# Expert gates of a PEER layer: from one-hot products to a scatter through DRAM, and part of one token tile's value product by gathered rows

## Chip, cores and metric

One core of one Trainium2 chip runs the whole kernel as one program. The metric is device time in microseconds (us) of a run, from several runs of the same compiled kernel.

## What is computed

The reference is one encoder block on 256 tokens of width 2048 in float32: a token-mixing sublayer (pooling, attention, gates), then a retrieval sublayer. The change is in the retrieval sublayer:

```python
q = jnp.einsum('bsd,de->bse', x, wq).reshape(B, S, PEER_HEADS, 2, PEER_HALF)      # 8 heads
s1 = jnp.einsum('bshc,kc->bshk', q[..., 0, :], keys1)                             # 128 keys each
s2 = jnp.einsum('bshc,kc->bshk', q[..., 1, :], keys2)
v1, i1 = lax.top_k(s1, 16);  v2, i2 = lax.top_k(s2, 16)
cand = v1[..., :, None] + v2[..., None, :]                                        # 256 candidates
vals, pos = lax.top_k(cand, 16)
ids = take_along_axis(i1 * 128 + i2, pos);  gates = softmax(vals)                 # 16 picks a head
h = jnp.einsum('td,tkd->tk', xb, u_tab[ids])
out = jnp.einsum('tk,tkd->td', gelu(h) * gates, v_tab[ids])                       # 128 picks a token
```

The kernel computes the two last lines densely: h for all 16,384 experts and all 256 tokens, gelu, a multiplication by a gate matrix that is zero where a token did not pick the expert (gates of one expert picked by several heads add up), and a product with the whole of v_tab.

## The kernel before

**Units.** All weights stream from HBM in units of 128 x 1024 float32 (512 KB). SyncE loads unit u into one of four RAW slots once DVE has converted unit u - 4 (load, L302); ACT rounds it to float32r into HI (L436); DVE writes the rest, RAW - HI, into LO (conv, L720; two slots, so the conversion of u waits for the end of unit u - 2); TensorE multiplies hi by hi, hi by lo and lo by hi (use, L1178 on). The order is written out by hand: while TensorE does unit n, ACT converts n + 3 and DVE n + 1. The 774 units come in stages: v, qk, pool, gate, grp, branch, wout, plew, wq, pleg, u (256 units), vtab (256 units).

**t_unit** (L1194, L1195, L1199) keeps weights stationary: 16 hi matmuls and 8 lo matmuls with 256 token columns each. **n_unit** (L1212, L1219) keeps tokens stationary: a unit is one half (1024 columns) of a row block, and does for each of two token tiles two hi passes and one lo pass over two 512-column pieces: 8 + 4 matmuls of 512 columns.

**u stage.** Two units give one "chunk" of 128 experts (one value of i2, all i1): h for 128 experts x 256 tokens in PSUM. ACT applies gelu into BUF[:, k, :] (L650) for the first 64 chunks, while DVE does the top-k searches, one step tk0 to tk7 behind each conversion (L978 to L1041). After 64 chunks the picks are turned by TensorE, and for the last 64 chunks each unit is followed by the one-hot products of two tokens: DVE builds two one-hot tiles per token (onehots, L1079, L1081), TensorE multiplies them (gate_products, L1448) into the token's 128 x 128 gate matrix, and DVE multiplies BUF with it (spread, L1092, L1096). Chunks not yet reached hold 1.0, which two POOL memsets wrote (L410, L412).

**vtab stage.** For each key k ACT and DVE split BUF[:, k, :] into a_hi and a_lo (L683, L1131), and n_unit multiplies with the 128 rows v_tab[:, k, :], two units (halves) per key, adding up in all eight PSUM banks until the end.

**POOL** also scales the residual and adds the gated embedding (L403 to L407), stores it in DRAM (L408) and brings it back in pieces late in vtab (L421, L423). DVE then adds it, and the last layer norm follows. In the pool stage DVE sums windows (pool_sums, L818) in buffers that lie where the change puts its zeros.

## Time and profile before

| | us |
|---|---|
| median of 3 runs | 2414.81 (2414.21 to 2416.8) |
| the profiled execution's own time | 2416.51 |
| its span, first to last instruction | 2414.8 |
| TensorE busy | 2307.8 (96%) |
| DVE busy | 1538.1 (64%) |
| ACT busy | 1028.5 (43%) |
| POOL busy | 72.5 (3%) |

The granted TensorE clock is 0.982 of full speed on average. The queue of SyncE moved 412.14 MB (54.1% of the time of the 16 DMA engines), the queue of POOL 12.71 MB; the mean over the span is 176 GB/s. Shares are means over stages; a busy TensorE means that matmuls followed one another, not that each ran at its peak. A duration of an engine's instruction includes pipelining, so that neighbours overlap by a few hundredths of a us.

### The profile page before, as it was taken

How to read it: one execution, taken by the hardware profiler on the slowest of the kernel's cores; microseconds unless marked ns; L12 is line 12 of the kernel's file. 1: busy time of each engine (PE TensorE's matmuls, PEld its weight loads, DVE VectorE, ACT ScalarE, POOL GpSimd, SP SyncE). 2: the span in 40 equal slices, each digit the busy share in tenths (PEclk: the TensorE clock that was granted, in tenths of full speed). 3: DMA queues.
4: the chain of work that ended last, by engine and by line, in shares of the span. 5: the costliest groups of instructions: out<-in, count | busy, mean ns of one | idle time of the engine just before them, and what ended most of it. 6: DMA issues, size and time to landing. Idle time of an engine off the chain costs nothing.

```text
span 2414.8 us, 45807 instructions
## 1 busy us (share of the span) xinstructions
PE 2307.8 (96%) x15504; PEld 2135.9 (88%) x15504; DVE 1538.1 (64%) x2726; ACT 1028.5 (43%) x1390; POOL 72.5 (3%) x64
## 2 busy tenths in 40 slices
PE   4999999899899989999999999999999999999996
PEld 4999999897699879999999999999788888888885
DVE  4446655565653568777779898989555555555556
ACT  2444455554444443444443333333444444444442
POOL 0000000000010040000000000000000000000000
PEclk9999999999999999999999999999999999999998
DMA  6655555455544555555554445444566666666663
GB/s 178 189 182 164 172 178 168 155 181 177 192 142 156 187 166 172 182 182 182 181 177 131 160 157 159 157 157 157 182 193 194 202 205 201 201 202 202 206 193 123
DMA packets 116576, 425.28 MB, mean 176 GB/s; under 512 B 13840, under 2 KB 13856, under 8 KB 115520
## 3 DMA queue, kind: packets, MB, share of 16 engines
q1 hardware_dynamic: 112608, 412.14, 54.1%
q0 software_dynamic: 3936, 12.71, 2.2%
q8 instruction: 20, 0.33, 0.1%
q14 instruction: 12, 0.10, 0.0%
HBM read 418.50 MB, written 6.29 MB: 176 GB/s over the span
## 4 chain that ended last, share of the span: by engine, by line
PE 90%; DVE 5%; DMA 3%; issue 1%; ACT 1%; DVEq 0%; SPq 0%; ACTq 0%
PE ps L1212 24%; PE ps L1199 17%; PE ps L1194 17%; PE ps L1195 17%; PE ps L1219 12%; PE ps L1448 2%; DMA raw<-in_w_in 2%; DVE w_lo L720 1%; DMA ln_gb<-in_ln_in 1%; DVE bn L733 0%; DVE x L739 0%; DVE tk_ab L1022 0%; PE ps L1320 0%; PE ps L1390 0%; DVE x L745 0%
## 5 line engine op out<-in xcount | busy, mean ns | idle before, releaser
L720 DVE TENSOR_TENSOR w_lo<-raw,w_hi 128x1024 fp32r<-128x1024 f32 x774 | 957.7, 1239 | 713.7 <-PE ps L1219 418.0
L436 ACT ACTIVATE w_hi<-raw 128x1024 fp32r<-128x1024 f32 x774 | 820.5, 1061 | 1061.2 <-DMA raw<-in_peer_v 384.2
L1194 PE MATMUL ps<-x_t_hi,w_hi 128*128 128x256 f32 x3328 | 835.9, 289 | 21.0 <-ACT v_t L486 12.5
L1195 PE MATMUL ps<-x_t_lo,w_hi 128*128 128x256 f32 x3328 | 820.9, 284 | 0.0
L1194 PEld LDWEIGHTS ps<-x_t_hi,w_hi 128*128 128x128 f32 x3328 | 641.7, 193 | 25.9 <-ACT w_hi L436 15.9
L1195 PEld LDWEIGHTS ps<-x_t_lo,w_hi 128*128 128x128 f32 x3328 | 642.4, 193 | 0.0
L1199 PE MATMUL ps<-x_t_hi,w_lo 128*128 128x256 f32 x3328 | 472.1, 285 | 13.5 <-DVE w_lo L720 13.5
L1199 PEld LDWEIGHTS ps<-x_t_hi,w_lo 128*128 128x128 f32 x3328 | 433.3, 194 | 14.8 <-DVE w_lo L720 14.7
L1212 PE MATMUL ps<-w_hi,x_t_hi 128*128 128x512 f32 x1024 | 315.8, 390 | 3.0 <-DVE x_t_lo L1131 3.0
L1212 PE MATMUL ps<-w_hi,x_t_lo 128*128 128x512 f32 x1024 | 316.1, 390 | 0.0
L1219 PE MATMUL ps<-w_lo,x_t_hi 128*128 128x512 f32 x1024 | 274.1, 389 | 0.0
L1212 PEld LDWEIGHTS ps<-w_hi,x_t_hi 128*128 128x128 f32 x1024 | 192.5, 188 | 43.1 <-issue 3.2
L1219 PEld LDWEIGHTS ps<-w_lo,x_t_hi 128*128 128x128 f32 x1024 | 192.6, 188 | 40.2
L1212 PEld LDWEIGHTS ps<-w_hi,x_t_lo 128*128 128x128 f32 x1024 | 192.5, 188 | 40.1
L1096 DVE TENSOR_TENSOR experts<-ps,experts 128x512 f32 (+1 forms) x64 | 87.6, 1369 | 13.2 <-DVE experts L1092 13.1
L1212 PE MATMUL ps<-w_hi,a_hi 128*128 128x512 f32 x272 | 87.5, 403 | 7.7 <-DVE a_lo L932 3.7
L1081 DVE TENSOR_SCALAR onehots<-iota,i_t,gate_t 128x128 f32<-128x128 bf16 x256 | 92.6, 362 | 0.0
L1079 DVE TENSOR_SCALAR onehots<-iota,i_t 128x128 f32<-128x128 bf16 x256 | 77.5, 303 | 17.7 <-DVE experts L1096 13.2
L1212 PE MATMUL ps<-w_hi,a_lo 128*128 128x512 f32 x272 | 87.4, 403 | 0.0
L1448 PE MATMUL ps<-onehots 128*128 128x128 f32 x512 | 79.0, 277 | 5.2 <-DVE onehots L1081 5.2
L1219 PE MATMUL ps<-w_lo,a_hi 128*128 128x512 f32 x272 | 75.3, 399 | 0.0
L1448 PEld LDWEIGHTS ps<-onehots 128*128 128x128 f32 x512 | 69.3, 194 | 5.6 <-DVE onehots L1081 5.6
(204 smaller groups left out, 1313.8 us busy)
## 6 DMA issues: line engine op xcount, KB each, us to landing
raw<-in_u SPq DMA_DIRECT2D x256, 512.0 KB, 4.6
raw<-in_peer_v SPq DMA_DIRECT2D x256, 512.0 KB, 4.9
raw<-in_w_in SPq DMA_DIRECT2D x128, 512.0 KB, 4.6
raw<-in_branch SPq DMA_DIRECT2D x32, 512.0 KB, 3.9
raw<-in_wout SPq DMA_DIRECT2D x32, 512.0 KB, 3.7
raw<-in_wq SPq DMA_DIRECT2D x32, 512.0 KB, 3.8
raw<-in_pleg SPq DMA_DIRECT2D x32, 512.0 KB, 3.8
x<-in_x SPq DMA_DIRECT2D x2, 1024.0 KB, 6.2
```

Of the source, the lines that this page charges most:

```text
L436: nc.scalar.activation(HI[:, u % 4, :], RAW[:, u % 4, :], ACT.Copy).then_inc(hi_ready, 1)
L720: v.tensor_tensor(LO[:, u % 2, :], RAW[:, u % 4, :], HI[:, u % 4, :].bitcast(F32), ALU.subtract) \
L1079: ch.tag(v.tensor_scalar(OH[:, j % 2, r, 0, :], IOTA[:, :], I1T[:, bass.ds(t, 1)], None, ALU.is_equal))
L1081: ins = v.tensor_scalar(OH[:, j % 2, r, 1, :], IOTA[:, :], I2T[:, bass.ds(t, 1)], GATET[:, bass.ds(t, 1)], ALU.is_equal, ALU.mult)
L1096: v.tensor_tensor(dst, PS[:, 4 + c, :].rearrange("p (t e) -> p t e", t=4), dst, ALU.mult) \
L1194: mm(o, w(HI, u % 4)[:, k, :], xh[:, ks * half + k, :], start=(s and k == 0), stop=False)
L1195: mm(o, w(HI, u % 4)[:, k, :], xl[:, ks * half + k, :], start=False, stop=False)
L1199: r = mm(o, w(LO, u % 2)[:, k, :], xh[:, ks * half + k, :], start=False, stop=(e and k == 7))
L1212: mm(nbank(tt, 2 * half + q), stn[:, tt * P:(tt + 1) * P], HI[:, u % 4, q * 512:(q + 1) * 512], start=(first and s == 0), stop=False, skip ...
L1219: r = mm(nbank(tt, 2 * half + q), ah[:, tt * P:(tt + 1) * P], LO[:, u % 2, q * 512:(q + 1) * 512], start=False, stop=last, skip_group_chec ...
L1448: r = mm(PS[:, 4 + c, o:o + P], OH[:, j % 2, t, 0, :], OH[:, j % 2, t, 1, :], start=True, stop=True)
```

## The change

**Search.** The top-k search does both token tiles at once, in 16 stages per head (tk0 to tk15), one behind each conversion from unit 7 of wq on; products and index arithmetic are on floats. It yields cell addresses (ID, in SBUF) for the two tiles and row addresses (IDV) for the second.

**Gates.** In three batches of heads (0 to 2, 3 and 4, 5 to 7), ACT exponentiates, DVE normalises, and then DVE sums for every pick the gates of equal cells over the heads up to that batch's end: one scalar_tensor_tensor with accumulation per pick and tile, five behind a conversion (merge_gates). As equal cells get their sum, POOL scatters the sums plainly: per head and tile 16 indirect DMAs of 128 cells of 4 bytes into a gate array of 8 MB per tile in DRAM. That array is set to zero by 16 DMAs of POOL from the start of qk on. pool_sums waits for the last of them.

**u stage.** All 128 chunks go through gelu on ACT, which also writes the second tile's half of each to DRAM (64 KB). The one-hots, their products, the spreading, the turned picks and the memsets of 1.0 are gone. At unit 192 SyncE waits until all is scattered, and then reads the gates of a chunk back (two DMAs of 64 KB) into three slots, behind the load of the unit; DVE multiplies two chunks behind each conversion from step 196 on, and the last eight after the last conversion.

**vtab stage.** For the second token tile the last 768 columns are left out of the dense product: odd units do 6 matmuls of 512 columns and 3 of 256. In their place POOL gathers, for each of 128 picks, a row piece of 768 columns for each of the tile's 128 tokens, and the gelu value of the pick; DVE multiplies and adds into ACC, spread over keys 10 to 127. The residual comes back in 1 MB pieces at pick 64. DVE's loops over u and vtab are written out.

```diff
+PICKS = HEADS * TOPK
+BATCHES = ((0, 3), (3, 5), (5, 8))
...
+G_SLOTS = 3
+GC = 768
+DC = D - GC
+REST = DC - UNIT
+ROWS = 7
+PICKS_FROM = 10
+G_FROM = 195
...
+def gated_by(n):
+
+    return max(0, min((n - G_FROM) * 2, n // 2 - 2))
...
+            def chunk_gates(k):
+
+                if k >= G_SLOTS:
+                    sp.wait_ge(g_mult, k - G_SLOTS + 1)
+                for tt in range(NT):
+                    sp.dma_start(GR[:, k % G_SLOTS, tt * P:(tt + 1) * P], gates_dram[tt][k]
+                                 ).then_inc(g_in[k % G_SLOTS], 16)
...
+                if name == "vtab":
+                    for j in range(4):
+                        load(None, 4, b + j, src(name, None, j // 2, j % 2))
+                        for k in range(gated_by(2 * NK - 5 + j), gated_by(2 * NK - 4 + j)):
+                            chunk_gates(k)
+                    for k in range(gated_by(2 * NK - 1), NK):
+                        chunk_gates(k)
+                    first = 1
...
+                if name != "u":
+                    continue
+                for tt in range(NT):
+                    sp.wait_ge(scattered[tt], 16 * PICKS)
+                for j in range(4 * last, 2 * n):
+                    load(None, 4, b + j, src(name, None, j // 2, j % 2))
+                    for k in range(gated_by(j - 5), gated_by(j - 4)):
+                        chunk_gates(k)
...
+            pool.wait_ge(zero_ready, 1)
+            pool.wait_ge(unit_done, BASE["qk"])
+            for n in range(16):
+                pool.dma_start(gates_dram[n // 8][n % 8 * 16:n % 8 * 16 + 16].rearrange("k p e -> p k e"), ZERO[:, :, :]
+                               ).then_inc(zero_out, 16)
...
-            pool.wait_ge(n_act, 16)
+            cells = [gates_dram[tt].rearrange("k p t -> (k p t)").unsqueeze(1) for tt in range(NT)]
+            def residual():
+                pool.wait_ge(n_act, 16)
+                for tt in range(NT):
+                    step(nc.gpsimd.tensor_tensor(SIG[:, tt, :], SIG[:, tt, :], PW[:, tt, :], ALU.mult))
+                    step(nc.gpsimd.tensor_tensor(X0[:, tt, :], X0[:, tt, :], SIG[:, tt, :], ALU.add))
+                    pool.dma_start(spill[tt], X0[:, tt, :]).then_inc(spill_out, 16)
...
+            pool.wait_ge(zero_out, 16 * 16)
+            for h0, h1 in BATCHES:
+                for h in range(h0, h1):
+                    pool.wait_ge(gates_ready, h + 1)
+                    for tt in range(NT):
+                        if h:
+                            pool.wait_ge(scattered[tt], 16 * TOPK * h)
+                        for p in range(TOPK * h, TOPK * (h + 1)):
+                            pool.indirect_dma_start(out=cells[tt], out_offset=bass.IndirectOffsetOnAxis(
+                                ap=ID[:, tt, p:p + 1], axis=0), in_=GSC[:, tt, p:p + 1], in_offset=None
+                                ).then_inc(scattered[tt], 16)
+                    if h == 0:
+                        residual()
             for tt in range(NT):
...
+                pool.wait_ge(scattered[tt], 16 * PICKS)
+            hidden_cells = hidden.rearrange("k p t -> (k p t)").unsqueeze(1)
+            table = a["peer_v"].rearrange("a b (c d) -> (a b c) d", d=256)
+            for n in range(4):
+                pool.wait_ge(h_out[n], 16 * NK // 4)
+
+            def picked(p):
+                pool.indirect_dma_start(out=HP[:, p:p + 1], out_offset=None, in_=hidden_cells,
+                                        in_offset=bass.IndirectOffsetOnAxis(ap=ID[:, 1, p:p + 1], axis=0)
+                                        ).then_inc(h_in[p // TOPK % 2], 16)
+
+            for p in range(TOPK):
+                picked(p)
+            pool.wait_ge(unit_done, BASE["vtab"])
+            for p in range(PICKS):
+                if p >= ROWS:
+                    pool.wait_ge(row_used, p - ROWS + 1)
+                pool.indirect_dma_start(out=ROW[p % ROWS][:, :], out_offset=None, in_=table,
+                                        in_offset=bass.IndirectOffsetOnAxis(ap=IDV[:, p:p + 1], axis=0)
+                                        ).then_inc(row_in[p % ROWS], 16)
+                if p + TOPK < PICKS:
+                    picked(p + TOPK)
+                if p == 64:
+                    pool.wait_ge(al_ready, KD + 2 + KD + 32)
+                    for tt in range(NT):
+                        pool.dma_start(RES2[:, tt, :], spill[tt]).then_inc(res_in, 16)
+                    for x in range(2):
+                        pool.dma_start(LNG2[:, x, :], bass.AP(tensor=a["ln2"].tensor, offset=x * D,
+                                                              ap=[[0, P], [1, D]])).then_inc(ln_in[2], 16)
...
+                    act.wait_ge(act_evac, val(i, 4, 80 + c + 1))
+                    if i is not None:
+                        act.wait_ge(h_out[c], i * 16)
+                    nc.scalar.dma_start(hidden[k].rearrange("k p t -> (k p) t"),
+                                        BUF[:, k, P:S].rearrange("p k t -> p (k t)")).then_inc(h_out[c], 16)
...
+                act.wait_ge(g_mult, val(i, 4, c + 1))
...
-                dve.wait_ge(const_ready, 3)
+                dve.wait_ge(const_ready, 4)
...
+            scores = lambda h, tt, f: SC[:, 2 * h + tt, f, :]
+            first = lambda h: slice(TOPK * h, TOPK * h + 8)
+            second = lambda h: slice(TOPK * h + 8, TOPK * (h + 1))
+
...
+            def merge_gates(b, n):
+
+                h0, h1 = BATCHES[b]
                 ch.wait()
...
+                if (NT * TOPK * h0 + 5 * n) // (NT * TOPK):
+                    dve.wait_ge(gates_ready, (NT * TOPK * h0 + 5 * n) // (NT * TOPK))
+                for m in range(NT * TOPK * h0 + 5 * n, min(NT * TOPK * h0 + 5 * n + 5, NT * TOPK * h1)):
+                    h, tt, p = m // (NT * TOPK), m // TOPK % NT, m // (NT * TOPK) * TOPK + m % TOPK
+                    width = TOPK * h1
+                    ins = v.scalar_tensor_tensor(out=SAME[:, m % 5, 0:width], in0=IDF[:, tt, 0:width],
+                                                 scalar=IDF[:, tt, p:p + 1], in1=GATE[:, tt, 0:width],
+                                                 op0=ALU.is_equal, op1=ALU.mult, accum_out=GSC[:, tt, p:p + 1])
+                    if m % (NT * TOPK) == NT * TOPK - 1:
+                        ins.then_inc(gates_ready, 1)
+                    else:
                         ch.tag(ins)
...
+            def gated(k):
+
+                dve.wait_ge(h_out[k % 4], 16 * (k // 4 + 1))
+                dve.wait_ge(g_in[k % G_SLOTS], 16 * NT * (k // G_SLOTS + 1))
+                v.tensor_tensor(BUF[:, k, :], BUF[:, k, :], GR[:, k % G_SLOTS, :], ALU.mult).then_inc(g_mult, 1)
+
+            st = stage("pleg", KD + 2, gt_block, AH, AL)
+            for n in range(32):
+                conv(None, 4, BASE["wq"] + n + DVE_LEAD)
+                search(n - 7)
+            for n in range(32):
+                if n % 2 == 0:
+                    st(None, n // 2)
+                conv(None, 4, BASE["pleg"] + n + DVE_LEAD)
+                if n < 27:
+                    search(25 + n)
+                elif n == 27:
+                    gates_out(0)
+                else:
+                    merge_gates(0, n - 28)
+            done, found = 0, 52
+            for n in range(2 * NK):
+                conv(None, 4, BASE["u"] + n + DVE_LEAD)
+                if n == 53:
+                    gates_out(1)
+                if n == 117:
+                    gates_out(2)
+                if n < 16:
+                    merge_gates(0, 4 + n)
+                elif 54 <= n < 67:
+                    merge_gates(1, n - 54)
+                elif 118 <= n < 138:
+                    merge_gates(2, n - 118)
+                elif found <= STAGES * HEADS:
+                    search(found)
+                    found += 1
+                for k in range(done, gated_by(n)):
+                    gated(k)
+                done = gated_by(n)
+            for k in range(done, NK):
+                gated(k)
...
+            def pick(p):
+
+                g = p // TOPK
+                if p % TOPK == 0:
+                    sl = slice(p, p + TOPK)
+                    dve.wait_ge(h_in[g % 2], 16 * TOPK * (g // 2 + 1))
+                    ch.link(v.tensor_tensor(HP[:, sl], HP[:, sl], GATE[:, 1, sl], ALU.mult))
+                dve.wait_ge(row_in[p % ROWS], 16 * (p // ROWS + 1))
+                if p == 0:
+                    ins = v.tensor_scalar(ACC[:, :], ROW[0][:, :], HP[:, 0:1], None, ALU.mult)
+                else:
+                    dve.wait_ge(row_used, p)
+                    ins = v.scalar_tensor_tensor(out=ACC[:, :], in0=ROW[p % ROWS][:, :], scalar=HP[:, p:p + 1],
+                                                 in1=ACC[:, :], op0=ALU.mult, op1=ALU.add)
+                ins.then_inc(row_used, 1)
...
+                upto = max(0, (k - PICKS_FROM + 1) * PICKS // (NK - PICKS_FROM))
+                if made < upto:
+                    pick(made)
+                    made += 1
+                if k + 2 < NK:
+                    a_lo(None, k + 2)
+                if k + 1 < NK:
+                    conv(None, 8, vb + 2 * k + 1 + DVE_LEAD)
+                while made < upto:
+                    pick(made)
+                    made += 1
+
+
+            dve.wait_ge(res_in, 16 * 2)
+            dve.wait_ge(row_used, PICKS)
+            ch.tag(v.tensor_tensor(RES2[:, 1, DC:D], RES2[:, 1, DC:D], ACC[:, :], ALU.add))
+            dve.wait_ge(ln_in[2], 16 * 2)
             for half in range(2):
 
                 dve.wait_ge(unit_done, UNITS - 1 + half)
                 for tt in range(NT):
...
             for tt in range(NT):
                 stats(RES2, tt)
@@ -1205,19 +1361,24 @@
 
                 half = u % 2
 
+                def pieces(tt):
+                    if u >= BASE["vtab"] and half and tt:
+                        return [(q, min(512, REST - 512 * q)) for q in range(2) if REST > 512 * q]
+                    return [(0, 512), (1, 512)]
+
                 def his():
                     for tt in range(NT):
                         for s, stn in enumerate((ah, al)):
-                            for q in range(2):
-                                mm(nbank(tt, 2 * half + q), stn[:, tt * P:(tt + 1) * P],
-                                   HI[:, u % 4, q * 512:(q + 1) * 512], start=(first and s == 0), stop=False,
+                            for q, w in pieces(tt):
+                                mm(nbank(tt, 2 * half + q)[:, 0:w], stn[:, tt * P:(tt + 1) * P],
+                                   HI[:, u % 4, q * 512:q * 512 + w], start=(first and s == 0), stop=False,
                                    skip_group_check=True)
 
                 def los():
                     for tt in range(NT):
-                        for q in range(2):
...
                         pe.wait_ge(act_evac, i * 4 + (80 + j // 2 - 1))
 
                         pe.wait_ge(n_act, 12 if j == 0 else 16)
                     t_unit(i, 8, BASE["u"] + j, 2 * (j // 2 % 2), j % 2, XH, XL)
-            pe.wait_ge(act_evac, 80 + TOPK_CHUNKS)
-
```

## Rows read from the trace of the kernel before

**Rows 1.** Windows: stretch, its length; busy us (instructions) per engine; PEclk, DMA share, GB/s
```profile
10.00:20.00 10.00, 0.01 (x1) 0.00 (x0) 7.38 (x12) 3.10 (x4) 0.00 (x0) 1.00 0.95 384
...
910.00:1240.00 330.00, 330.00 (x2739) 330.00 (x2739) 261.18 (x847) 139.92 (x171) 0.00 (x0) 0.99 0.58 183
...
1275.00:1690.00 415.00, 414.02 (x3490) 413.83 (x3490) 373.70 (x752) 153.15 (x185) 0.00 (x0) 1.00 0.50 157
...
1705.00:2380.00 675.00, 675.00 (x2980) 558.92 (x2979) 346.09 (x373) 300.62 (x372) 8.60 (x16) 1.00 0.65 199
```

**Rows 2.** Chain of waits, pieces at seams: start us, us, what
```profile
871.36 0.38 PE ps L1194
...
909.51 2.08 PE ps L1199 x8
...
1257.10 0.97 PE ps L1199 x8
...
1690.18 0.97 PE ps L1199 x8
...
1694.61 3.29 PE ps L1212 x8
...
1704.66 1.81 PE ps L1212 x8
1706.47 0.91 PE ps L1219 x4
```

**Rows 3.** DVE groups, whole span; the last one from 1720 to 2350 us only
```profile
L720 DVE TENSOR_TENSOR w_lo<-raw,w_hi 128x1024 fp32r<-128x1024 f32 x774 | 957.7, 1239 | 713.7 <-PE ps L1219 418.0 <-PE ps L1199 260.0 <-ACT w_hi L436 30.3
...
L1131 DVE TENSOR_TENSOR x_t_lo<-experts,x_t_hi 128x256 fp32r<-128x256 f32 x128 | 53.6, 419 | 1.1 <-ACT x_t_hi L683 1.1
...
L745 DVE SCALAR_TENSOR_TENSOR x<-x,rstd,ln_gb 128x1024 f32<-128x1024 f32 x8 | 9.7, 1282 | 0.1
...
L829 DVE SCALAR_TENSOR_TENSOR pool_w<-pool_w,pool_in 128x512 f32<-128x512 f32 x4 | 2.8, 692 | 0.1
...
L720 DVE TENSOR_TENSOR w_lo<-raw,w_hi 128x1024 fp32r<-128x1024 f32 x232 | 284.3, 1225 | 307.2 <-PE ps L1219 304.5 <-ACT w_hi L436 2.7
```

**Rows 4.** Timeline of POOL: start us, us, instruction
```profile
21.05 1.10 POOL L369 DMA_DIRECT2D bias_by_rel_dram<-bias_by_rel  x1 [14.72 <-ACT bias_by_rel L474]
...
884.32 4.58 POOL L406 TENSOR_TENSOR ple_gate<-ple_gate,p_w 128x2048 f32<-128x2048 f32 x1
...
899.13 8.63 POOL L410 MEMSET experts<- 128x10240 f32 x1 [3.82 <-DMA residual_dram<-x]
...
1903.24 0.54 POOL L421 DMA_DIRECT2D residual<-residual_dram  x1 [24.71 <-ACT x_t_hi L683]
```

**Rows 5.** DMA issues: queue, count, KB each, median us from issue to landing
```profile
raw<-in_u SPq DMA_DIRECT2D x256, 512.0 KB, 4.6
raw<-in_peer_v SPq DMA_DIRECT2D x256, 512.0 KB, 4.9
...
ln_gb<-in_ln_in SPq DMA_DIRECT2D x2, 1024.0 KB, 12.1
bias_by_rel_dram<-bias_by_rel POOLq DMA_DIRECT2D x1, 2048.0 KB, 46.2
...
bias<-bias_by_rel_dram POOLq DMA_DIRECT2D x8, 64.0 KB, 2.1
```

**Rows 6.** Chain of waits early in the v stage
```profile
36.74 30.21 DMA raw<-in_w_in
```

**Rows 7.** Timeline of DVE beside the POOL operations of rows 4
```profile
885.72 4.28 DVE L720 TENSOR_TENSOR w_lo<-raw,w_hi 128x1024 fp32r<-128x1024 f32 x1
...
899.97 7.82 DVE L1021 TENSOR_SCALAR tk_ab<-tk_pos 128x16 uint32<-128x16 uint32 x1
...
1903.32 1.23 DVE L720 TENSOR_TENSOR w_lo<-raw,w_hi 128x1024 fp32r<-128x1024 f32 x1 [1.50 <-PE ps L1219]
```

More of the change, by code:

```diff
@@ L436, in conv, with run @@
                 nc.scalar.activation(HI[:, u % 4, :], RAW[:, u % 4, :], ACT.Copy).then_inc(hi_ready, 1)
-            def run(name, iters, per, slots, pre=None, start=0, stop=None):
+            def run(name, iters, per, slots, pre=None, start=0, stop=None, peel=False):
                 b = BASE[name]
@@ L966, in _ @@
             xt_lo(1)
-            run("wq", 8, 4, {})
-            run("pleg", 8, 4, {}, pre=stage("pleg", KD + 2, gt_block, AH, AL))
             def settle():
```

425 lines of the change are left out of this document (184 added, 241 removed).

## Prediction, made before the change was run

> **What bounds the kernel now.** I read the table of windows first [rows 1]. In the three long stretches TensorE (PE) is busy for all but 1 us in 1,420, and at the full granted clock; VectorE (DVE) is busy 79% of the first half of the u stage, 90% of its second half and 51% of the vtab stage. The chain of waits [rows 2] gives the periods. In vtab a unit is 8 matmuls in 1.81 us and 4 in 0.91 us: 2.72 us, or 227 ns for 512 columns. In the first half of u, the 120 units between the ends at 911.59 (909.51 + 2.08) and 1258.07 (1257.10 + 0.97) take 2.887 us each, or 120 ns for a matmul of 256 columns. The two sizes are 107 ns apart, so a column costs 0.417 ns and a matmul 13 ns besides. The second half of u (128 units up to 1691.15) takes 3.38 us a unit, because two tokens' one-hot products follow every unit. So the kernel is bound by matmul columns, except at seams. PE stands between 1691.15 and 1694.61, and the first 8 units of u, from 871.36 to 911.59, take 40.2 us where 8 periods are 23.1: 17 us lost.
>
> **Term 1, one-hot products go.** The second half of u with its seam ran 1258.07 to 1691.15, 433.1 us; 128 units at 2.887 us are 369.5. Gain **63.6 us**. The one-hots, the spreading multiply and the transposes of the picks go with it.
>
> **Term 2, columns go in vtab.** Each odd unit loses three 512-column matmuls (680 ns), and three shrink from 512 to 256 columns (3 x 107 = 320 ns): 1.00 us per key. 128 keys give **128 us**, and a key (two units) then takes 5.44 - 1.00 = 4.44 us. This is the gain only if nothing else needs over 4.44 us.
>
> DVE in vtab [rows 3]: two conversions of 1.239 us, one a_lo of 0.419, and 1.085 gathered multiply-adds per key (128 spread over 118 keys). Its scalar_tensor_tensor took 692 ns for 512 and 1,282 ns for 1,024 columns, so 987 ns for 768. Sum 2.48 + 0.42 + 1.07 = 3.97 us of 4.44. Of the 307 us that DVE idled before its conversions in that stage, 304.5 were for PE, so it has room, though after the change only a tenth.
>
> DMA in vtab: a key's loads are 1.049 MB and its 1.085 rows of 128 x 3,072 bytes 0.427 MB: 1.475 MB in 4.44 us, 332 GB/s. The trace bounds the ceiling: 384 GB/s at 95% share between 10 and 20 us, and 199 GB/s at a share of 0.65, which stretched to 1.0 is 306 [rows 1]. At 384 it costs nothing; at 306 a key takes 4.82 us, 118 x 0.38 = 45 us. The first row is a rate that was reached, the second only a proportion, so I take **+15 us**, a third of the way.
>
> **Term 3, gates by scatter.** POOL issues 256 scatters of 128 cells in u, and in vtab 128 row gathers and 112 one-word gathers (16 before them). No row has an indirect DMA. The nearest are plain ones: 0.54 us on POOL for one of 128 rows, 1.10 us for one of 1,024 [rows 4]; none bounds it from above, which is rival B. I take 1.1 us. In vtab 2.17 per key need 2.4 of 4.44 us. In u the last three heads become ready from step 124 on, and SP holds its loads at step 192 until all has landed: 96 scatters in about 64 x 2.887 = 185 us, so 1.9 us each is allowed. Cover for both: nothing.
>
> DVE in u: search and merging. The largest step is a 1,024-element operation beside the conversion, 2 x 1.24 = 2.48 us of 2.887; a merge step has five 128-wide instructions of some 0.25 us (by the same line), 1.25 + 1.24. Nothing; cover some 0.4 us a unit, and in pleg less. ACT's 128 writes of 64 KB and its table loads lie in ACT's idle time.
>
> **Term 4, the zero fill.** 16 DMAs write 16.8 MB from the start of qk, and pool_sums waits for the last some 35 units later: 35 x 2.887 = 101 us, 166 GB/s beside loads of 183. The sum, 349, lies under 384. Below: nothing. Above: a 2 MB write from POOL landed after 46.2 us [rows 5] and a load beside it held the chain for 30.2 us [rows 6], though that write reads only eight partitions. I take **+8 us** (0 to 40).
>
> **Term 5, start of u.** POOL's four large tensor operations and a memset held DVE: a conversion took 4.28 us beside a 4.58 us POOL operation and a 16-element tensor_scalar 7.82 us beside an 8.63 us memset [rows 4, 7]. The memsets of 1.0 go, the four operations move behind the 32 scatters of head 0, beside search steps. I keep two thirds of the 17 us: **-5 us** (0 to -10).
>
> **Term 6, gate reads in the tail of u.** This is what hides badly. In steps 196 to 255 DVE multiplies two chunks per unit; their four reads of 64 KB stand on SP's queue right behind the 512 KB load of the same step, in three slots. The load goes out when a conversion ends (time x); the chunks are wanted after the next conversion. Let L be the time until they have landed and P the period. DVE then multiplies twice (0.84), converts (1.24) and spends some 0.1 on waits, and this must end at x + 2P: 2P = L + 2.2. P stays 2.887 if L is under 3.6 us. Bounds for L: a 64 KB read on POOL's queue lands in 2.1 us, a load of u in 4.6 [rows 5]. On one queue later ones do land later: the ln_gb rows, issued behind two x loads, took 12.1 us. I take the load's 4.6 + 0.3: P = 3.55, 60 x 0.66 = **+40 us** (0 to 60). The last eight chunks come after the last step, three slots per round of 2.1 us of landing, 0.42 of multiplying and some waits, about 3 us: 8 us in all, then a_lo(0): the stop of 3.46 us between u and vtab grows to some 13: **+10 us**.
>
> The Trainium skill (DMA: Bandwidth & Descriptors, Queues, rings and completion order) says that each DMA engine consumes one ring's descriptors in order. By that rule L is the load's own landing and more, and the term stands; without it L would be the lone 64 KB read's and the term zero. The ln_gb row agrees with the rule.
>
> At the end, the gathered sum's add goes before the last units are ready and two adds shrink: nothing.
>
> **Sum.** 2414.8 (span) - 63.6 - 128 + 15 + 8 - 5 + 40 + 10 = 2291. The profiled execution took 2416.5 us around its span of 2414.8; the median of the runs is 2414.81, the span by chance, so the sum is taken for the median: **2290 us**. About 0.2% (5 us) is what a measurement tells from no change.
>
> **Rivals.**
> A. *Indirect DMAs hold DVE* (ends slower). For: a POOL tensor operation kept a two-input DVE operation waiting until it ended [rows 4, 7]. Against: a plain POOL DMA from 1903.24 to 1903.78 left the conversion begun at 1903.32 at its usual 1.23 us. If each held DVE for h us: in vtab (taking 0.08 us off each instruction where they overlap) 3.7 + 2.17h against 4.44, over 118 keys; in u 1.35h against some 0.5 us of room over 190 units. That is 118 x (2.17h - 0.74) + 190 x (1.35h - 0.5), or 512h - 182: with h = 1.1, 381 us, 2670 us in all. It decides from h = 0.6 on. Chance 0.10.
> The Trainium skill (SBUF — State Buffer, Who interferes with whom) says that a DVE instruction with two SBUF inputs contends with a GpSimd instruction that reads SBUF. An indirect DMA reads its offsets there, so this rule speaks against the change; the POOL tensor operations agree with it, and no row shows an indirect DMA.
> B. *POOL is too slow.* At t us per indirect DMA: 256 x (t - 2.05) in vtab and 96 x (t - 1.9) before step 192; t = 2.5 gives 173 us, 2463 us. Slower from 2.3 us on. For: nothing measured; against: 0.54 and 1.10. Chance 0.06.
> C. *DMA becomes vtab's bound.* At 306 GB/s 30 us more than summed, 2320; at 270 GB/s a key takes 5.46 us, 120 us in place of 15: 2395. For: loads of peer_v already land later than those of u (4.9 against 4.6 us, [rows 5]) and gathers are shorter; against: 384. Chance 0.22.
> D. *The gate reads are hidden*: L under 3.6, the fill free, 384 GB/s: 2290 - 40 - 8 - 15 = 2227 us. Chance 0.14.
>
> **How the numbers follow.** Forecast 0.48, within 2250 to 2350. Those 0.48, C and D are faster; A and B mostly slower, with a sliver around no change and a piece of them (h near 0.5) still faster. Faster 0.82, same 0.03, slower 0.15. The range, 2225 to 2430, reaches over D, C and the first of B, and leaves out A with some of B.
>
> **What the profile would show.** Term 1: 24-matmul units at 2.88 us through u up to step 195. Term 2: odd vtab units at 1.72 us, PE at 100%; if DVE is longer than 1.24 us in its conversions, A; if ACT waits for raw<-in_peer_v before PE stands, C; if DVE waits for rows while DMA has room, B. Term 6: DVE before the chunk multiply waiting for DMA, P near 3.5 us. Term 4: ACT waiting for raw in qk, or DVE for zero_out. I am wrong if u's tail runs at 2.88 us, or if vtab's keys differ from 4.44 us by over 0.3.

## The result, and the profile after

The changed kernel was timed in four sets of executions, each beside the kernel before. They don't agree:

| set | changed kernel, us | before beside it, us | ratio, 95% interval |
|---|---|---|---|
| first (the one that the prediction was made for) | 2571.77 median of 4 (2527.32 to 2588.30) | 2415.81 | 1.0524 [1.0415, 1.0633] |
| second (e9) | 2292.61 median of 5 (2289.75 to 2294.55) | 2413.61 | 0.9495 [0.9482, 0.9507] |
| third (e12) | 2287.44 median of 4 (2284.63 to 2287.80) | 2414.44 | 0.9472 [0.9456, 0.9488] |
| fourth (e18) | 2289.06 median of 2 (2287.12 to 2291.01) | 2414.76 | 0.9480 [0.9461, 0.9499] |

In the first set the executions of 2585.74 and 2588.30 us count as slow, and the ratio is that of the two others (2527.32 and 2557.81 us).

The prediction was 2290 (2225 to 2430), faster. Against the first set it is wrong in sign and 282 us off; the three later ones, of the same kernel unedited, lie within 3 us of it. The three later sets ran on three different chips of this kind; on which the first ran is not recorded. The edited kernels below ran in these sets and in two more, on two further chips. So there are two questions: what took 280 us in the first set, and whether 2290 came out for the right reasons.

**Where the first set's time went.** Windows of its profile (stretch, its length; busy us and instructions of PE, PEld, DVE, ACT, POOL; PEclk, DMA share, GB/s):

```profile
100.00:200.00 100.00, 100.00 (x837) 100.00 (x836) 41.67 (x34) 43.07 (x60) 14.41 (x14) 1.00 0.95 346
...
940.00:1000.00 60.00, 27.99 (x154) 24.25 (x154) 22.65 (x71) 6.33 (x8) 48.04 (x41) 0.67 0.32 98
1000.00:1034.00 34.00, 4.71 (x13) 3.44 (x12) 2.09 (x5) 1.06 (x1) 26.04 (x27) 0.50 0.06 16
1050.00:1150.00 100.00, 100.00 (x836) 100.00 (x835) 76.28 (x209) 46.11 (x55) 0.00 (x0) 1.00 0.63 194
1400.00:1480.00 80.00, 34.44 (x164) 27.95 (x163) 14.75 (x66) 7.13 (x8) 61.65 (x61) 0.61 0.16 45
```

Read PE against POOL: where POOL has nothing to do (1050 to 1150) TensorE is busy all the time, as before; in the worst stretch of POOL's scatters (1000 to 1034) it gets 13 matmuls done in 34 us. Inside such a stretch the timeline shows each of them by itself (start, us, instruction, idle time before it):

```profile
1466.23 0.37 PE L1355 MATMUL ps<-x_t_hi,w_lo 128*128 128x256 f32 x1 [1.73 <-issue]
1467.22 0.96 POOL L479 DMA_INDIRECT gates_dram<-cell_gates,cell_ids  x1 [0.30 <-issue]
1468.32 0.29 PEld L1355 LDWEIGHTS ps<-x_t_hi,w_lo 128*128 128x128 f32 x1 [3.21 <-issue]
1468.49 0.97 POOL L479 DMA_INDIRECT gates_dram<-cell_gates,cell_ids  x1 [0.30 <-issue]
1469.03 0.37 PE L1355 MATMUL ps<-x_t_hi,w_lo 128*128 128x256 f32 x1 [2.43 <-issue]
```

These are matmuls of the same unit on operands that are long there; no semaphore stands between them. PE waits 1.7 to 2.4 us ahead of nearly each with nothing in the profile to wait for ("issue"), while POOL's scatters keep their steady 1.27 us (0.97 and 0.30), and the DMA engines are nearly idle. The granted clock is down at 0.50 there (the 1.2 GHz level), after PE had been waiting; a matmul takes 0.37 us instead of some 0.28. DVE's longest waits from 900 to 1550 us name no one the profile knows ("remote"); its ordinary wait, for PE, stands below them:

```profile
DVE w_lo L815 <- remote: 250.5, 23, 46.6
DVE w_lo L815 <- PE ps L1355: 88.5, 99, 2.7
```

(us in total, times, longest.) The slowness doesn't begin with a burst. POOL issues the first scatter of the third burst at 1395.50; PE keeps its pace of 0.12 us a matmul for 14 us and ten scatters, and this is its first stop:

```profile
1409.78 0.28 PE L1351 MATMUL ps<-x_t_lo,w_hi 128*128 128x256 f32 x1 [0.35 <-issue]
```

From there the stops grow. POOL issues the last scatter of head 6 at 1479.94, and from 1490 on PE is busy all the time again, until head 7's scatters slow it in the same way.

From 874.9 to the end of its last matmul at 1905.5, u took 1031 us; in e12 it took 783. These 248 us, and some 20 at the start of vtab, where POOL's gathers come in a burst and the chain holds 6.95, 5.09 and 12.45 us of "another core or an unknown queue" between 1928 and 1956, are but for 3 us the whole difference of the two spans (2556.1 against 2285.4). I call it the crawl.

**The same kernel without it.** Windows of e12, columns as above; POOL's scatters fill 1275 to 1375 in just the same way, and PE does not notice:

```profile
875.00:975.00 100.00, 93.86 (x765) 93.05 (x764) 81.77 (x250) 40.19 (x50) 78.69 (x55) 0.98 0.63 194
...
1275.00:1375.00 100.00, 100.00 (x836) 100.00 (x835) 43.59 (x41) 43.74 (x53) 78.75 (x70) 1.00 0.65 194
...
1450.00:1650.00 200.00, 177.02 (x1374) 167.33 (x1374) 111.19 (x171) 67.75 (x86) 0.00 (x0) 1.00 0.78 232
...
1690.00:2190.00 500.00, 490.24 (x2262) 400.54 (x2261) 394.01 (x439) 257.58 (x324) 282.99 (x229) 1.00 0.92 324
...
1860.00:1960.00 100.00, 99.38 (x463) 81.72 (x462) 82.21 (x92) 51.91 (x66) 60.54 (x48) 1.00 0.91 323
1960.00:2060.00 100.00, 92.69 (x417) 74.26 (x416) 73.35 (x82) 47.92 (x60) 56.44 (x48) 0.98 0.91 333
2060.00:2160.00 100.00, 99.30 (x464) 82.04 (x464) 82.10 (x92) 52.73 (x66) 59.17 (x47) 1.00 0.92 326
```

Its chain of waits (start, us, what), at the start of u, in u's tail, at the seam and at the end:

```profile
870.48 1.58 ACT ple_gate L741 x3
...
1562.74 1.23 DVE w_lo L815
1563.99 0.33 SPq L327
...
1564.37 0.43 SPq L334
...
1564.84 4.10 DMA gate_chunks<-gates_dram
...
1569.03 0.44 DVE experts L1221
...
1569.48 0.32 SPq L334
...
1569.85 2.65 DMA gate_chunks<-gates_dram
...
1572.93 1.23 DVE w_lo L815
...
1653.49 1.23 PE ps L1355 x8
...
1655.59 0.38 ACT experts L749
1655.96 12.07 issue
1668.03 3.75 PE ps L1373 x8
...
2257.02 0.60 PE ps L1380 x3
```

With [rows 2] and the last unit of before (which ended at 2392.8) this gives the budget, stage by stage:

| stretch | before | e12 | difference | predicted |
|---|---|---|---|---|
| to the first matmul of u | 871.4 | 872.1 | +0.7 | +8 |
| u | 819.8 | 782.7 | -37.1 | -28.6 |
| stop between u and vtab | 3.5 | 13.3 | +9.8 | +10 |
| vtab | 698.2 | 589.6 | -108.6 | -113 |
| from the last matmul | 22.0 | 27.8 | +5.8 | 0 |
| span | 2414.8 | 2285.4 | -129.4 | -123.6 |

### The profile page after: what moved, and what is told of

Its sections match the earlier page's. It is cut to its first block, busy times and chain, and to the rows that moved or that the text cites. A ratio compares the mean times of both kernels' runs of the same rounds, so it can differ in the third digit from the quotient of the medians.

```text
span 2556.1 us, 43127 instructions
## 1 busy us (share of the span) xinstructions
PE 2224.6 (87%) x14602; PEld 2024.9 (79%) x14602; DVE 1504.5 (59%) x2630; ACT 1028.1 (40%) x1395; POOL 649.1 (25%) x580
## 4 chain that ended last, share of the span: by engine, by line
PE 63%; DMA 13%; issue 11%; DVE 8%; ACT 2%; another core or an unknown queue 1%; SPq 1%; ACTq 0%; DVEq 0%
PE ps L1355 15%; PE ps L1350 15%; PE ps L1351 15%; PE ps L1373 11%; DMA raw<-in_peer_v 6%; PE ps L1380 6%; DVE w_lo L815 4%; DMA gate_chunks<-gates_dram 3%; DMA raw<-in_w_in 1%; DMA raw<-in_u 1%; ACT w_hi L524 1%; DMA ln_gb<-in_ln_in 1%; SPq L327 0%; DVE same_cell L1201 0%
## 5 line engine op out<-in xcount | busy, mean ns | idle before, releaser
L815 DVE TENSOR_TENSOR w_lo<-raw,w_hi 128x1024 fp32r<-128x1024 f32 x774 | 949.0, 1234 | 762.1 <-PE ps L1355 345.1
L479 POOL DMA_INDIRECT gates_dram<-cell_gates,cell_ids x256 | 268.6, 1049 | 573.2 <-DVE same_cell L1201 495.1
L1373 PE MATMUL ps<-w_hi,x_t_hi 128*128 128x512 f32 (+1 forms) x896 | 279.3, 382 | 22.1 <-issue 14.1
L1373 PE MATMUL ps<-w_hi,x_t_lo 128*128 128x512 f32 (+1 forms) x896 | 270.3, 378 | 0.0
L492 POOL DMA_INDIRECT picked<-hidden_dram,cell_ids x128 | 165.3, 1292 | 405.7 <-DMA hidden_dram<-experts 365.5
L1380 PE MATMUL ps<-w_lo,x_t_hi 128*128 128x512 f32 (+1 forms) x896 | 237.1, 381 | 16.7 <-DVE w_lo L815 9.8
L502 POOL DMA_INDIRECT row<-in_peer_v,row_ids x128 | 143.3, 1119 | 243.1 <-DVE gathered_sum L1279 194.5
L749 ACT ACTIVATE experts<-ps 128x256 f32 (+1 forms) x128 | 48.6, 380 | 299.3 <-remote 154.1
L1279 DVE SCALAR_TENSOR_TENSOR gathered_sum<-row,picked,gathered_sum 128x768 f32<-128x768 f32 x127 | 128.8, 1014 | 0.3
L1221 DVE TENSOR_TENSOR experts<-experts,gate_chunks 128x256 f32<-128x256 f32 x128 | 53.2, 426 | 101.4 <-DMA gate_chunks<-gates_dram 94.2
L1264 DVE TENSOR_TENSOR x_t_lo<-experts,x_t_hi 128x256 fp32r<-128x256 f32 x128 | 54.4, 426 | 80.0 <-ACT x_t_hi L781 60.7
```

The costliest lines, as they stand in the source:

```text
L479: pool.indirect_dma_start(out=cells[tt], out_offset=bass.IndirectOffsetOnAxis(ap=ID[:, tt, p:p + 1], axis=0), in_=GSC[:, tt, p:p + 1], in_ ...
L492: pool.indirect_dma_start(out=HP[:, p:p + 1], out_offset=None, in_=hidden_cells, in_offset=bass.IndirectOffsetOnAxis(ap=ID[:, 1, p:p + 1], ...
L502: pool.indirect_dma_start(out=ROW[p % ROWS][:, :], out_offset=None, in_=table, in_offset=bass.IndirectOffsetOnAxis(ap=IDV[:, p:p + 1], axis=0)
L815: v.tensor_tensor(LO[:, u % 2, :], RAW[:, u % 4, :], HI[:, u % 4, :].bitcast(F32), ALU.subtract) \
L1264: v.tensor_tensor(XL[:, c % 4, :], BUF[:, bass.ds(val(i, 4, c), 1), :].rearrange("p a t -> p (a t)"), XH[:, c % 4, :].bitcast(F32), ALU.su ...
L1279: ins = v.scalar_tensor_tensor(out=ACC[:, :], in0=ROW[p % ROWS][:, :], scalar=HP[:, p:p + 1], in1=ACC[:, :], op0=ALU.mult, op1=ALU.add)
```

## Experiments

All edits are to the changed kernel. The first four were chosen to take the crawl apart, before it was known that it need not show.

**e1, no scatters.**

```diff
-                            pool.indirect_dma_start(out=cells[tt], ..., in_=GSC[:, tt, p:p + 1], in_offset=None
-                                ).then_inc(scattered[tt], 16)
```

> Left out: the 256 scatters of single gates into DRAM and the waits for them; the gates that are read back are zeros. All else is as in the changed kernel. Theory S (the bursts of scatters make TensorE crawl in the u stage): the stalls at 900 to 1040, 1170 to 1260 and 1395 to 1545 us vanish, u runs at 2.88 us a unit up to step 195, and the time falls from 2572 to 2290 to 2340 us (the predicted 2290 plus the 20 to 45 us lost at the start of vtab, where gathers come in a burst). Rival T (the longer search and merge steps of DVE, or the residual's four operations on POOL, hold the chain, and the scatters only stand beside it): the time stays within 30 us of 2572.

Measured: 2295.8 us (2286.2 to 2298.9), ratio 0.9506 [0.9479, 0.9533].

**e2, a shorter loop on TensorE.**

```diff
-            with pe.Fori(0, 32) as i:
-                for j in range(8):
+            with pe.Fori(0, 64) as i:
+                for j in range(4):
```

> The same instructions in the same order; only TensorE's loop over u holds 4 units (64 passes) in place of 8 (32 passes). Theory F (during a burst TensorE waits for its own instructions, which a loop body of 192 matmuls has fetched anew in every pass): with half the body the issue time ahead of matmuls in the bursts goes, and the time falls to 2300 to 2400 us. Rival B (what is slow is the way out of the engine, its semaphore increments, or the DMA's transfers themselves): no change, 2540 to 2590 us, with the same crawl in the windows 980 to 1020 and 1440 to 1480.

Measured: 2280.9 us, PE at 100% through every burst. It looked like a full confirmation of theory F.

**e3, one scatter in flight.**

```diff
+                            if p:
+                                pool.wait_ge(scattered[tt], 16 * p)
```

> Each scatter waits until the one before it has landed. Theory Q (the scatters pile up: POOL issues one per 1.27 us, faster than 128 single cells drain, and the backlog blocks what TensorE needs): there is never more than one in flight, the crawl is gone or small, each scatter takes some 3 us from issue to landing, and the time falls under 2400 us, unless the 96 last ones (96 x 3 = 290 us from step 124 on) hold the loads at step 192, which adds up to 100 us there. Rival R (each scatter costs TensorE a fixed time whatever their spacing): total loss as before, spread thin, 2540 to 2600 us.

Measured: 2638.3 us, and not by a crawl. Windows of e3:

```profile
1180.00:1380.00 200.00, 200.00 (x1669) 200.00 (x1669) 117.95 (x284) 89.91 (x108) 58.54 (x45) 1.00 0.63 194
1460.00:1760.00 300.00, 0.00 (x0) 0.00 (x0) 0.00 (x0) 0.00 (x0) 123.08 (x128) 0.50 0.01 0
```

PE runs clean while scatters go, and then stands still, because SyncE and ACT wait for all of them. In the second line 128 scatters take 300 us with nothing beside them: one per 2.3 us, and the chain has 2.17 us from issue to landing. Beside loads the chain shows 2.6 to 5.9 us, mostly near 5. The expectation bounded the stop at 100 us from 3 us a scatter; with some 5 us a scatter ahead of it, the stop was 334 us.

**e4, gathers in place of scatters.**

```diff
-                            pool.indirect_dma_start(out=cells[tt], out_offset=..., in_=GSC[:, tt, p:p + 1], in_offset=None
+                            pool.indirect_dma_start(out=GR[:, tt, p:p + 1], out_offset=None, in_=cells[tt], in_offset=...
```

> Each scatter is replaced by a gather of the same 128 cells of 4 bytes into on-chip memory; the gate array stays zero, so the gates read back are zeros. Theory W (it is the scattered writes to DRAM that are slow): the crawl goes and the time is that of the kernel without scatters, 2290 to 2340 us. Rival D (it is the many small descriptors of an indirect DMA, whichever way they go; the burst of gathers at the start of vtab is the same thing): the crawl stays, 2500 to 2600 us.

Measured: 2287.0 us.

**e5, a longer loop**, and **e6, plain writes.**

```diff
-            with pe.Fori(0, 32) as i:
-                for j in range(8):
+            with pe.Fori(0, 16) as i:
+                for j in range(16):
```

> As the changed kernel, but TensorE's loop over u holds 16 units (16 passes) in place of 8. Theory F (a body that is too long is fetched anew in every pass, and the scatters hold up the fetches; 4 units fit, 8 don't): as many instructions per unit have to come as with 8, so the crawl is as in the changed kernel: 2500 to 2620 us. Rival A (the 8-unit body happened to lie or branch badly, and any other body mends it): 2275 to 2300 us as with 4 units. Rival J (the cost is at the jump back, once per pass): half the passes, half the loss, about 2420 us.

```diff
-                            pool.indirect_dma_start(out=cells[tt], ...
+                            pool.dma_start(gates_dram[tt][p][:, p:p + 1], GSC[:, tt, p:p + 1]
```

> As the changed kernel with the 8-unit body, but each scatter is a plain DMA of POOL that writes the same 128 words of 4 bytes to fixed places 512 bytes apart (chunk p, column p), so the gates are wrong; no address is read from on-chip memory. Theory W (small writes to DRAM hold up the fetch of TensorE's instructions): the crawl stays, 2450 to 2650 us. Rival D (it takes the indirect form, whose descriptors are made from addresses that the engine reads): the crawl goes, 2280 to 2310 us.

Measured: e5 2289.8, e6 2302.1 us. e5 is against theory F: a body of twice the length, fetched from the same place, did not crawl. That left "8 units and scatters of single cells, and nothing else", which is an odd cause, and the unedited kernel had not been run beside any of these.

**e9, the changed kernel unedited; e10, e11.** e10 is the 8-unit body with the tail of e8 (below), e11 is e2 again.

> The changed kernel, nothing edited. Theory K (the crawl belongs to the kernel: the 8-unit body together with scatters of single cells, since other bodies, gathers and plain writes did not show it): 2530 to 2590 us again. Rival M (the crawl belongs to the first set of executions, by the chip or by where the program's memory lay there, and each of the other runs was free of it for that reason alone): 2280 to 2300 us.

> The 8-unit body again, with the tail that gave 2255 us with the 4-unit body (chunk reads on POOL's queue, four slots, from step 185 on). Theory K: the crawl is back and costs some 280 us, 2500 to 2560 us. Rival M: 2250 to 2265 us, the body doesn't matter.

> The changed kernel with the 4-unit body, as once before (2280.9 us in one run). Under either theory 2275 to 2300 us; theory K has it 280 us under the unedited kernel beside it, rival M level with it, within 10 us.

Measured: e9 2292.6, e11 2292.2, e10 2259.0 us (2253.0 to 2268.8). Theory K falls, rival M stands (it is what is left, not what was shown): e9 and e11 are level, and neither body length nor the kind of transfer had anything to show. With that e1 to e6 lose their meaning for the crawl (there was none to take away) and keep only their times: all but e3 lie within 2281 to 2302, so the scatters themselves cost next to nothing (e1 2295.8 without them, e9 2292.6 with them), as the prediction had it.

**e12, e18, the kernel unedited twice more.**

> The changed kernel once more, unedited, in another set of executions. Theory M (the crawl belongs to the condition of one set of executions, which only kernels that scatter feel, since the kernel before ran at its usual 2415 there): either level is possible, 2285 to 2300 us or 2525 to 2590 us, but nothing between; if the crawl shows, the kernels beside it tell whether fewer scatters in flight mend it.

> The changed kernel unedited, in a fourth set. Either 2285 to 2300 us, or the crawl's 2525 to 2590 us. After two sets at the lower level I expect the lower.

Measured: 2287.4 and 2289.1 us.

**e7 and e8, the tail of u.** Both have the 4-unit body. e7 moves the 256 chunk reads from SyncE's queue to POOL's; e8 also adds a fourth slot and starts the multiplications at step 185.

```diff
+            for k in range(NK):
+                if k >= G_SLOTS:
+                    pool.wait_ge(g_mult, k - G_SLOTS + 1)
+                for tt in range(NT):
+                    pool.dma_start(GR[:, k % G_SLOTS, tt * P:(tt + 1) * P], gates_dram[tt][k]
+                                   ).then_inc(g_in[k % G_SLOTS], 16)
```

```diff
-G_SLOTS = 3
-G_FROM = 195
+G_SLOTS = 4
+G_FROM = 185
```

> The 4-unit body, and the gate chunks are read on POOL's queue instead of SyncE's behind the loads; three slots as before, the same steps. In the 4-unit kernel the tail of u ran 87.7 and 83.6 us of TensorE in two stretches of 100 us, and stood for 12 us after it. Theory L (the chunk reads land 4.4 us after issue because the load of 512 KB stands ahead of them on the same queue): they land in 2 to 3 us, the tail of u runs at 2.9 to 3.0 us a unit, and 30 us are gained: 2250 us. Rival V (DVE's own work, 1.24 + 2 x 0.42 us with its waits, makes the period): no gain, 2275 to 2290 us.

> As the run before it, with a fourth slot for gate chunks, and the multiplications start at step 185 in place of 195, so that three chunks are left after the last conversion in place of eight. If the reads' place on the queue was all, the tail is clean already and this gains only the shorter stop between u and vtab: 12 us less 3, about 5 to 9 us more than the run before it, 2240 to 2245 us. If three slots on POOL's queue still leave DVE waiting (two chunks per unit, each read some 3.2 us from slot free to landed), this gains 15 to 30 us over it.

Measured: e7 2298.0 us (2293.8 to 2303.6), no gain; e8 2255.0 (2251.2 to 2262.8). The chain of waits of e7:

```profile
1560.68 0.43 DVE experts L1206
1561.11 0.28 issue
1561.39 0.53 POOL gate_chunks L469
1561.92 3.52 DMA gate_chunks<-gates_dram
...
1565.88 1.03 DVE w_lo L800
...
1567.72 0.53 POOL gate_chunks L469
1568.25 4.18 DMA gate_chunks<-gates_dram
```

On a queue without loads a 64 KB read of the chain still lands in 3.5 to 4.2 us, much as behind the load (4.10 in e12's chain); over all 256 reads the medians are 3.4 us in e7 and 3.3 in e12. Its place on SyncE's queue is not what makes it late. What e7's chain shows in its place is the round through three slots: read, multiply, slot free, issue, read. (POOL takes 0.53 us to issue a read, SyncE 0.32 or 0.43, so e7 gave a little away there.) In e8 reads of the chain take even 4.7 to 5.1 us, and PE hardly notices. Windows of e8, and its chain at the seam:

```profile
1440.00:1540.00 100.00, 98.02 (x811) 97.21 (x810) 63.13 (x98) 39.95 (x50) 69.21 (x132) 1.00 0.84 269
```

```profile
1625.64 0.97 PE ps L1341 x8
...
1627.12 4.16 issue
1631.29 3.75 PE ps L1359 x8
```

811 matmuls in 100 us are 2.96 us a unit. In that stretch DVE multiplies two chunks per unit as in e7, so the earlier start is not what shortened the unit; the fourth slot is what differs. The stop of PE between u and vtab (13.3 us in e12) is 4.7 us, from 1626.6 to 1631.29. Four slots on SyncE's queue, and either edit of e8 without the other, were not run.

**e13, e14, e15, beside one another.** e13 is e8 with the residual's operations on POOL in pieces; e14 is e8 with few scatters in flight; e15 is e8 again.

```diff
-                    if h == 0:
-                        residual()
+                            if h in (1, 2) and p % 4 == 3:
+                                residual(8 * (h - 1) + 4 * tt + p % TOPK // 4)
```

```diff
-                    for tt in range(NT):
-                        if h:
-                            pool.wait_ge(scattered[tt], 16 * TOPK * h)
-                        for p in range(TOPK * h, TOPK * (h + 1)):
+                    for n in range(TOPK):
+                        tt, p0 = n % 2, TOPK * h + n // 2 * 2
+                        if p0:
+                            pool.wait_ge(scattered[tt], 16 * p0)
+                        for p in (p0, p0 + 1):
```

> The version of 2255 us, with the residual's four operations of 4.6 us on POOL cut into sixteen of 512 columns, one after every fourth scatter of heads 1 and 2. Theory H (a POOL operation holds DVE's conversion for its whole length, which costs the first 100 us of u 8 us of TensorE): each holds it for 1.2 us only, within DVE's room, and 4 to 8 us are gained, 2247 to 2251 us. Rival (what DVE loses is the sum of the holds, in however many pieces): no gain, within 3 us of the version beside it.

> The version of 2255 us (4-unit body, chunk reads on POOL's queue, four slots, from step 185), with the scatters issued two of a tile at a time, tiles in turn, so that four at most are in flight in place of some thirty. A pair's landing of some 5 us lies beside the other tile's pair (2.5 us of issue), so a scatter takes 1.3 to 1.8 us; the last 96 need at most 170 us and have 140 before step 185 asks for them. If the crawl does not show: 2250 to 2275 us. If it shows: theory Q (backlog) has this one free of it, rival R (each scatter costs) has it at 2500 or more.

> The version of 2255 us unedited, as the measure for the two beside it: 2250 to 2265 us without the crawl.

Measured: e13 2248.8 us (2241.2 to 2252.3; ratio 0.9320 [0.9304, 0.9335]), e15 2253.8 (2251.8 to 2261.7; 0.9343 [0.9323, 0.9364]), e14 2261.3 (0.9366). The medians of e13 and e15 are 5 us apart, as theory H has it, but their intervals overlap; the stretch itself decides. Windows of e15, then of e13:

```profile
860.00:960.00 100.00, 91.74 (x697) 88.17 (x697) 80.23 (x264) 42.16 (x52) 65.60 (x44) 0.98 0.62 188
```

```profile
860.00:960.00 100.00, 98.10 (x778) 95.73 (x777) 77.07 (x278) 48.15 (x60) 65.00 (x54) 1.00 0.61 185
```

PE is busy 6.4 us longer in it, and in the next 100 us, where most of the pieces now lie, both do 836 matmuls. A conversion beside a piece of 1.31 us took 2.36 or 3.09 us, one beside the whole operation up to 4.93 us (e12). e14 keeps four scatters at most in flight for 7 us more than e15; whether it is proof against the crawl could not be seen.

**e16 and e17, the gathered width**, on e13.

```diff
-GC = 768
+GC = 512    # e16;  e17: GC = 1024, ROWS = 5
```

> The version of 2249 us (residual in pieces), with 512 columns of the second tile gathered in place of 768. Theory P (in vtab TensorE's columns are the bound, as predicted): three matmuls of 256 columns grow to 512, 0.32 us a key, 41 us in 128 keys: 2285 to 2292 us. Rival C (the DMA rate is the bound there): a key moves 1.334 MB in place of 1.475, and 4.76 us of TensorE are the bound only just; 2262 to 2280 us if keys took over 4.55 us before.

> The same with 1024 columns gathered (odd units then do the first tile alone) and five row slots in place of seven. TensorE needs 4.08 us a key, DVE some 4.3 us (two conversions, a_lo, 1.085 multiply-adds of 1.29 us). Theory C' (at 768 columns the DMA engines stand at their ceiling of about 350 GB/s): 1.618 MB a key take 4.62 us or more, and the time is 2265 to 2290 us, slower. Rival P' (they have room up to the 384 GB/s seen at the start of the kernel): 4.3 us a key, 2228 to 2235 us.

Measured: 2262.2 and 2266.4 us against 2248.8. Windows of vtab in e13, e16, e17:

```profile
1690.00:2190.00 500.00, 489.75 (x2260) 398.41 (x2259) 400.47 (x446) 257.73 (x324) 282.22 (x222) 1.00 0.93 327
```

```profile
1690.00:2190.00 500.00, 497.49 (x2191) 410.59 (x2190) 366.70 (x433) 253.34 (x313) 254.90 (x220) 1.00 0.86 286
```

```profile
1690.00:2190.00 500.00, 463.26 (x1865) 339.60 (x1865) 415.47 (x430) 248.88 (x312) 287.44 (x221) 0.99 0.96 343
```

A key has 21 matmuls in the first two and 18 in the third, so keys take 4.65, 4.79 and 4.83 us, against 4.44, 4.76 and 4.08 of pure TensorE. At 512 columns TensorE is the bound (99.5% busy), at 1024 the transfers are (343 GB/s at a share of 0.96; PE waits 32 us for ACT, and ACT 242 us for loads of peer_v; DVE never waits for a row, so the five slots don't bind), and 768 stands between: on average 0.2 us a key above TensorE's need. So e16 came out as rival C had it (2262 to 2280): the 41 us of theory P left out what the transfers already cost at 768. e17 came out as theory C' (2265 to 2290).

## Why the prediction came out as it did

**Against the first set: wrong, by term 3.** Its step "Cover for both: nothing" priced the scatters by POOL's own time, and that held: one per 1.27 us (0.97 and 0.30), where 1.1 was taken and 1.9 allowed. What it put at nothing without a reason is what a burst of them does to the other engines: in the first set TensorE and the semaphores' arrival slowed beside the bursts, which cost 248 us in u and some 20 in vtab in the profiled execution. (Of the other three only times and mean clocks are kept: 2527 to 2588 us and 0.923 to 0.936, against 0.982 or more in the later sets of the same kernel.) Why it happened stays open, see below. None of the rivals named this. Rival A (slower through the scatters) had the sign and a chance of 0.10, but the wrong victim: DVE's conversions kept their 1,234 ns mean even in the first set, against 1,239 [rows 3], and 35 conversions between the scatters of 1275 to 1375 in e12 took 1,226 ns each. Rival B fell too: POOL was never late.

Two slips of its own arithmetic are without weight here. By its formula rival B is slower from 2.36 us on, not 2.3, and its parts that are called faster (0.48, C and D) add up to 0.84, not 0.82.

**Against the three later sets: right, for the most part by its own sum** (budget above). That it came within 3 us is luck in part: the first stretch and u came out 7.3 and 8.5 us better than summed, vtab and the end 4.4 and 5.8 us worse.
- Term 1: a clean unit of u takes 2.87 us (836 matmuls in 100 us), as taken.
- Term 2: 109 us gained in vtab where 113 were summed. A key takes 4.64 us on average, and 19 us of the 128 were lost, where 15 were taken: rival C in part. The loss isn't even. From 1860 to 1960 and from 2060 to 2160 a key takes some 4.54 us (463 and 464 matmuls in 100 us); between them only 417 matmuls were done, some 10 us fewer, and there the residual and the last norm's weights come in (four DMAs of 1 MB from 1962.45 on; 389 GB/s from 1970 to 1990). The sum had no term for these 4 MB. DVE's multiply-add took 1,014 ns, the estimate was 987.
- Term 4: nothing, not 8. PE was busy 100.00 of 100 us under the zero fill, at 346 GB/s. The sum of 349 was carried, and the fear of the 46 us write did not come true.
- Term 5: the start of u still loses some 8 us, where 12 were left in the sum; with POOL's four operations in pieces (e13) 6.4 of them go.
- Term 6: the number was right, its reason only in part, so the match is partly luck. P measured 3.49 us (200 x 24 / 1374) against 3.55, and the stop 13.3 against 13. One link of e12's chain is as forecast: the conversion ends at 1563.97, the load and the read are issued, and the read has landed at 1568.94, 4.97 us later, where L was taken as 4.9. The next link is one that the formula left out: the multiplication at 1569.03 has to free a slot before SyncE issues the next read (1569.48), and the conversion at 1572.93 comes only behind that read. The reads are as late on POOL's queue (e7), and with a fourth slot the period falls though they are still late (e8). The ln_gb row (12.1 us) that was taken to show lateness behind earlier transfers shows it less than it seems: in the kernel before, two such reads of 1 MB on POOL's queue, issued at 636.6 and 637.2 with no x load ahead of them, took a median of 9.3 us, against 6.2 of the x loads.
- The end: 5.8 us that the prediction had at nothing. Two gathered multiply-adds (1.02 and 1.03 us) and the sum's add come after the last matmul, not before it as forecast.

The Trainium skill was cited on two points. On rings (DMA: Bandwidth & Descriptors, Queues, rings and completion order) the prediction made the reads' lateness hang on their place behind a load in one ring; in e7 they left that ring and took as long (a median of 3.4 us, against 3.3 in e12), so the order within one ring didn't decide here. The same section of the Trainium skill says that a semaphore increment lands only after every earlier write of that DMA engine, across its queues; that would make a read late on either queue, and e7 agrees with it. On ports (SBUF — State Buffer, Who interferes with whom) the trace agrees for POOL's tensor operations (4.93 us for a conversion beside one). For the indirect DMAs it is POOL that waits: in e12, from 1275 to 1375 us, a scatter that starts while no conversion runs takes 0.97 us and one that starts during a conversion 1.30, while the conversions keep their 1.23 us.

**Open.** Why the first set crawled. Shown is where (only beside bursts of small indirect DMAs), how (matmuls 0.7 to 2.8 us apart by "issue", waits on "remote"), and that the kernel before, run in the same set, was untouched (2415.8). By the times it came in 4 of 4 executions there, and in none of the three later sets, nor in ten edited versions with the same 256 scatters. A backlog of descriptors, instruction fetch and late semaphore writes are guesses that fit the trace. That PE kept its pace for the first ten scatters of a burst, and had it back some 10 us after the last, speaks for something that piles up; more isn't shown, as no experiment met the crawl.

## What to carry to other kernels

Before taking a surprising time apart by experiments, run the unedited kernel once more beside the first of them: six runs here "confirmed" and refuted theories on an effect that was not there in their sets. A burst of small indirect DMAs that costs nothing in one set can cost 12% in another, so a kernel that depends on them should be timed in several sets; few in flight cost 7 us here, and whether that protects is not shown. And when small reads arrive late, count the slots of the round they go through before moving them to another queue: the queue alone gave nothing, a fourth slot with an earlier start gave 43 us on top (e7 to e8). And count every transfer of a stage whose DMA engines are nearly full: 4 MB of residual and norm weights cost some 10 us here. The best version run (e13: 4-unit body, chunk reads on POOL's queue in four slots from step 185, the residual in pieces) takes 2248.8 us, 6.8% under the kernel before.

## What the runs showed of the hardware that I had not expected

- An engine can be held ahead of nearly every instruction with nothing it waits for in the profile, 1.7 to 2.4 us ahead of a matmul, while the DMA engines show a share of 0.06 and POOL keeps its pace (first set, one trace).
- A scatter of 128 cells of 4 bytes takes 2.17 us from issue to landing alone, and 2.6 to 5.9, mostly near 5, beside 194 GB/s of loads.
- Reads of 64 KB beside loads of 512 KB land after a median of 3.4 us from POOL's queue (e7) and 3.3 from SyncE's, behind the loads (e12).
- The DMA engines carried 346 GB/s over 100 us (share 0.95) and 343 over 500 us (0.96), and 389 over 20 us (0.99). At 327 GB/s and a share of 0.93 (e13) keys already took 0.2 us more than their matmuls on average.
- An indirect DMA on POOL that starts during a conversion of DVE takes 1.30 us in place of 0.97, and the conversion keeps its 1.23 us (e12).
